# A residual's affine placed inside the FFN, and the rotary product issued one block later

## What is computed

```python
x = _layernorm(DEEPNORM_ALPHA * x + gt1 * y, ln1_g[i], ln1_b[i])
x = _layernorm(DEEPNORM_ALPHA * x
               + gt2 * _swiglu(x * (1.0 + sc2) + sh2, ffn_w_gate[i], ffn_w_up[i], ffn_w_down[i]),
               ln2_g[i], ln2_b[i])
# _layernorm(x, g, b) = (x - mean) * rsqrt(var + eps) * g + b
# in the attention: q and k of the latent tokens get  x * cos + x_rot * sin
```

## Time and profile before

| | us |
|---|---|
| median of 3 runs | 4185.95 (4185.85 to 4187.7) |
| span of the profiled execution | 4179.4 |
| PE busy | 3880.4 |
| DVE busy | 2160.6 |
| ACT busy | 1670.0 |
| GpSimd busy | 617.0 |

### The profile page before, as it was taken

One profiled execution on the slowest core, in us unless ns is written; L12 is line 12 of the kernel. 1 busy time (PEld: TensorE's weight loads), 2 busy tenths in 40 slices (PEclk: granted clock), 3 DMA queues, 4 the chain that ended last, 5 costly groups with the idle time before them and its releaser, 6 DMA issues.

```text
span 4179.4 us, 67654 instructions
## 1 busy us (share of the span) xinstructions
PE 3880.4 (93%) x28266; PEld 3183.4 (76%) x28266; DVE 2160.6 (52%) x3078; ACT 1670.0 (40%) x2711; POOL 617.0 (15%) x676
## 2 busy tenths in 40 slices
PE   6999999789999989987999899999999998899999
PEld 4877777668888867756788675778888877778887
DVE  3667754753222453377324654555665428655564
ACT  4445455422112341264223336544334435544333
POOL 0045555421000001003000000000210003000120
PEclk9999999888999999999999899999999999999999
DMA  5243454321211121103232320222223230312332
GB/s 162 79 144 125 157 163 153 108 88 61 71 61 61 58 81 61 41 1 112 84 98 91 66 81 11 83 91 72 97 95 108 81 111 4 133 62 82 101 101 81
DMA packets 235991, 367.67 MB, mean 88 GB/s; under 512 B 9811, under 2 KB 142630, under 8 KB 235302
## 3 DMA queue, kind: packets, MB, share of 16 engines
q1 hardware_dynamic: 217200, 300.49, 21.8%
q0 software_dynamic: 17936, 62.70, 4.9%
q10 hardware_dynamic: 550, 0.17, 0.0%
HBM read 344.36 MB, written 18.96 MB: 87 GB/s over the span
## 4 chain that ended last, share of the span: by engine, by line
PE 75%; DVE 15%; ACT 7%; issue 2%; DMA 1%; ACTq 0%; POOL 0%; DVEq 0%; SPq 0%; POOLq 0%
PE psum L259 21%; PE psum L261 20%; PE psum L260 20%; PE psum L256 12%; DVE arena L289 4%; ACT arena L389 3%; PE psum L265 2%; DVE arena L299 2%; DVE rw L289 2%; DVE rx L383 2%; DVE arena L303 1%; ACT rw L393 1%; DVE arena L295 1%; DVE arena L315 1%; ACT rx L393 1%
## 5 line engine op out<-in xcount | busy, mean ns | idle before, releaser
L259 PE MATMUL psum<-rx,rw 128*128 128x512 f32 (+2 forms) x2864 | 1057.8, 369 | 47.0 <-DVE rx L383 28.2
L260 PE MATMUL psum<-rx,rw 128*128 128x512 f32 (+2 forms) x2864 | 1030.5, 360 | 0.0
L261 PE MATMUL psum<-rx,rw 128*128 128x512 f32 (+2 forms) x2864 | 1028.6, 359 | 0.0
L289 DVE TENSOR_TENSOR rw<-arena,rw 128x2048 fp32r<-128x2048 f32 (+3 forms) x266 | 549.8, 2067 | 811.5 <-ACT rw L393 802.1
L256 PE MATMUL psum<-arena 32*32 32x32 f32 (+10 forms) x12982 | 762.8, 247 | 112.8 <-ACT arena L393 41.2
L256 PEld LDWEIGHTS psum<-arena 32*32 32x32 f32 (+5 forms) x12982 | 580.6, 133 | 256.1 <-issue 84.8
L393 ACT ACTIVATE rw<-arena 128x2048 fp32r<-128x2048 f32 (+3 forms) x266 | 453.6, 1705 | 753.4 <-PE psum L261 737.6
L259 PE MATMUL psum<-rw,rx 128*128 128x512 f32 (+1 forms) x1720 | 680.9, 396 | 31.1 <-DVE rx L383 13.8
L259 PEld LDWEIGHTS psum<-rx,rw 128*128 128x128 f32 (+1 forms) x2864 | 550.6, 192 | 181.8 <-DVE rx L383 40.6
L260 PE MATMUL psum<-rw,rx 128*128 128x512 f32 (+1 forms) x1720 | 672.5, 391 | 0.0
L261 PE MATMUL psum<-rw,rx 128*128 128x512 f32 (+1 forms) x1720 | 672.3, 391 | 0.0
(11 more groups left out here) (73 smaller groups left out, 2216.6 us busy)
## 6 DMA issues: line engine op xcount, KB each, us to landing
arena<-in_ffn_w_up SPq DMA_DIRECT2D x66, 1024.0 KB, 5.0
arena<-in_ada_w SPq DMA_DIRECT2D x48, 1024.0 KB, 6.6
arena<-in_ffn_w_down SPq DMA_DIRECT2D x40, 1024.0 KB, 4.9
arena<-in_ffn_w_gate SPq DMA_DIRECT2D x22, 1024.0 KB, 5.1
arena<-in_dn_w_in SPq DMA_DIRECT2D x16, 1024.0 KB, 6.0
arena<-in_xa_w_kv SPq DMA_DIRECT2D x16, 1024.0 KB, 5.0
arena<-in_hgrn_w_in SPq DMA_DIRECT2D x16, 1024.0 KB, 5.4
arena<-in_da_w_in SPq DMA_DIRECT2D x12, 1024.0 KB, 5.0
```

What stands on the lines that cost most here:

```text
L259: self.e.matmul(out, l[0], r[0], start=start, stop=False)
L260: self.e.matmul(out, l[0], r[1], start=False, stop=False)
L261: return self.e.matmul(out, l[1], r[0], start=False, stop=stop)
L289: return self.e.tensor_tensor(out, a, b, op)
```

## The change

`res1` and `res3` are unchanged in content, but GpSimd waits for `g0_GT 4` or `g1_GT 4` in front of them. `res2` is done a row (128 tokens) at a time in the attention's projection: behind cosine 6, 8, 10 and 12 GpSimd loads row t of `x_s`, multiplies and adds, and stores it back; the later reload brings the finished rows. The rotary product of block n is issued behind the first segment of block n+1, that of block 15 behind the first four-column step of the V projection. `have` becomes a function that gives the key.

```diff
-    v.wait_ge(*K.at(have, t))
+    v.wait_ge(*K.at(*have(t)))
+RES = DW + 3456
+def res_row(K, t):
+    return K.mem(RES + t % 2 * 1024, 1024)
+def pool_res_row(g, K, t):
+    gain, bias = pair_of(K, RES + 2048)
+    x = res_row(K, t)
+    if t == 0:
+        g.wait_ge(*K.at("m3_lo", 15))
+        pool_ln_rows(g, K, ("ln_rows", 2), RES + 2048, "ln2", 0)
+    if t >= 2:
+        g.wait_ge(*K.at("res_st", t - 2))
+    g.load(("res_ld", t), [(x, K.x_s[:, t * 1024:(t + 1) * 1024])], f"res_ld{t % 2}")
+    if t == 0:
+        g.wait_ge(*K.at("ln_rows", 2))
+    g.wait_ge(*K.at("res_ld", t))
+    g.tt(x, x, gain, MUL).then_inc(*g.sig())
+    g.tt(x, x, bias, ADD).then_inc(*g.sig(("res_x", t)))
+    g.wait_ge(*K.at("res_x", t))
+    g.load(("res_st", t), [(K.x_s[:, t * 1024:(t + 1) * 1024], x)], f"res_st{t % 2}")
+def pe_da_rot(p, K, n):
+    cosT, sinT, rot, raw, tmp = rope_mem(K, n)
+    p.wait_ge(*K.at("da_raw", n))
+    b = p.bank("da_rot", n)
+    p.mm(b[:, :], rot, raw).then_inc(*p.sig(("da_rot", n)))
+    p.close("da_rot", n)
@@ pe_da_proj
-            if s == 0:
-                cosT, sinT, rot, raw, tmp = rope_mem(K, n)
-                p.wait_ge(*K.at("da_raw", n))
-                b = p.bank("da_rot", n)
-                p.mm(b[:, :], rot, raw).then_inc(*p.sig(("da_rot", n)))
-                p.close("da_rot", n)
-    for j in range(2):
-        pe_proj_tok(p, K, ("da_v", j), da[:, 2048 + j * 512:2560 + j * 512], None, range(6))
+            if s == 0 and n:
+                pe_da_rot(p, K, n - 1)
+    pe_proj_tok(p, K, ("da_v", 0), da[:, 2048:2560], None, range(6), None,
+                lambda kh, t: pe_da_rot(p, K, 15) if (kh, t) == (0, 0) else None)
+    pe_proj_tok(p, K, ("da_v", 1), da[:, 2560:3072], None, range(6))
@@ pool_da_proj
+        if n == 15:
+            for t in (2, 3):
+                g.wait_ge(*K.at("res_st", t))
         g.tt((KT if wk else QT)[:, f, 0:512], raw, cosT, MUL).then_inc(*g.sig(("da_cos", n)))
+        if n in (6, 8, 10, 12):
+            pool_res_row(g, K, n // 2 - 3)
@@ dve_program: have="res1" / "res2" / "res3" become
+            have=lambda t: ("res1", t)    # down0
+            have=lambda t: ("res2",)      # da_out
+            have=lambda t: ("res3", t)    # down1
@@ pool_program
+    g.wait_ge(*K.at("g0_GT", 4))
     pool_affine(g, K, "res1", range(6), ("ln_rows", 1), CO + C_ONE, lambda t: ("m2_read", t // 4), K.X)
...
-    pool_ln_rows(g, K, ("ln_rows", 2), WK + 7168, "ln2", 0)
-    g.load(("x2",), [(da_rows(K), K.x_s.rearrange("p (t n) -> p t n", n=1024))])
-    pool_affine(g, K, "res2", range(4), ("ln_rows", 2), WK + 7168, lambda t: ("x2",),
-                da_rows(K))
+    g.load(("res2",), [(da_rows(K), K.x_s.rearrange("p (t n) -> p t n", n=1024))])
...
+    g.wait_ge(*K.at("g1_GT", 4))
     pool_affine(g, K, "res3", range(4), ("ln_rows", 3), WK + 18432, lambda t: ("m4_read", t // 2), K.X)
```

More of the change, by code:

```diff
@@ L4683, in dve_program @@
     dve_out(v, K, "down0", 22, 6, swiglu_out(K, 6), pair_of(K, CO + C_ONE), after=dve_ln_after(v, K, "ln2", t3),
-            have="res1")
+            have=lambda t: ("res1", t))
     yield "b0"
@@ L4693, in dve_program @@
     dve_ln_cols(v, K, "m4", 2, 1, 24, 32)
-    dve_out(v, K, "da_out", 8, 4, gate=pair_of(K, WK + 6144), after=dve_ln_after(v, K, "ln3", t4), have="res2",
+    dve_out(v, K, "da_out", 8, 4, gate=pair_of(K, WK + 6144), after=dve_ln_after(v, K, "ln3", t4), have=lambda t: ("res2",),
             begun=1, old=da_rows(K))
@@ L4701, in dve_program @@
     v.wait_ge(*K.at("gate_rows", 1, 1))
-    dve_out(v, K, "down1", 22, 4, out, pair_of(K, WK + 17408), after=dve_last_norm(v, K, WK + 20480), made=1, have="res3",
+    dve_out(v, K, "down1", 22, 4, out, pair_of(K, WK + 17408), after=dve_last_norm(v, K, WK + 20480), made=1, have=lambda t: ("res3", t),
             late=True)
```

## The result

The changed kernel takes **4127.34 us** (median of 4 runs, 4123.37 to 4134.16), the kernel before 4186.82 us beside it (4185.85 to 4188.02): ratio 0.9865, interval 0.9852 to 0.9878. The forecast was 4141 us with a range of 4134 to 4156.

What follows compares the result with a forecast made beforehand. TensorE, busy 93% of the span, bounds the kernel, so only its waits or low clock pay. Gains 14.7 + 11.2 + 3.6 + 15.6 = 45.1 us off 4179.4 give 4134.3, with 6.5 around the span 4141 us; range 4134 to 4156.

Steps and rivals of the forecast that it cites:

- part 4: Attention projection: issuing each rotary product a block later hides its ACT copy; gain 15.6 us, bounds 11 and 17.
- Part 1: Turn m2: moving res1 out frees DVE's splits from GpSimd's products; gain 9.0 + 5.7 = 14.7 us.
- part 2: Turn m4: moving res3 out shortens two halves on PE's path; gain 11.2 us.
- Part 3: Output projection: moving res2 out removes two PE waits; gain 3.6 us, bounds 2 to 5.
- (a): FFNs: moved res1 and res3 products delay weight splits by 4.9 us against 6.0 us of cover; cost 0.
- (b): Attention projection: res2's row 0 takes GpSimd 13 to 18 us against 22 us of room; hidden by 4 to 9.
- (c): Output projection start: x_s load and five broadcasts leave together, some 22 us sooner; cost 0, at worst a few us.
- (d): DVE's extra waits per tile name things long done; possible DMA starvation adds 2.3 to 4.6 us to row 0, hidden.
- Rival 1: FFNs: splits lose their cover as the block moves along with the products; 20 us come back, 4161 us; 8%.
- Rival 4: Attention projection: res2's row trips on GpSimd hold up PE, making the kernel slower, 4196 us; 6%.
- Rival 3: Turns m2 and m4: GpSimd goes early or isn't the cause of slowness; 26 us not gained, 4167 us; 4%.
- Rival 2: Attention projection: low clock in block 1 and DVE's queue cut the rotary gain to 5 us, 4152 us; 12%.

Runs made afterwards that it cites:

- e2: The changed kernel run again with no edit: 4128.28 us, ratio 0.9866 to the kernel before.
- e7: The changed kernel run a third time with no edit: 4133.92 us, ratio 0.9877 to the kernel before.
- e3: The kernel before with only the rotary product issued one block later, the three affines unmoved: 4160.45 us, ratio 0.9944.
- e4: The changed kernel with the rotary product put back behind its own segment, so only the affines are moved: 4155.36 us, ratio 0.9931.
- e8: The kernel before with only the two GpSimd waits in front of res1 and res3 added: 4156.48 us, ratio 0.9932.
- e9: The kernel before with each 128x1024 GpSimd affine product and sum issued as two of 128x512, nothing moved: 4159.86 us, ratio 0.9945.
- e5: The changed kernel with the second half of turn m3 put ahead of block 2's rope on DVE: 4123.25 us, ratio 0.9853.

## Why the prediction was wrong

Two steps failed, and together they don't account for all of the miss.

**The first: "with 6.5 4141 us".** I took the distance between the one profiled span (4179.4) and the median of three runs (4185.95) as time around the span. It is 1.8 us in every run whose span is on record. The other 4.7 us are the scatter between executions of one kernel. The 42 later runs of the kernel before have a median of 4182.7 and reach from 4175.8 to 4188.7. The profiled one, at about 4181.2 with 1.8 us around it, was a little quick, and the median of the three that I started from lay 3.3 us higher than that of the 42. With 1.8 the forecast would have been 4136, from the median of the 42 runs 4138. I gave the range no room for this, since three runs lay within 1.9 us.

**The second: the sum, 45.1, of which part 4 had 15.6.** The stages give 47.8 to 51.0 us, and part 4 gives 20.2. The term that failed is the eleven waits of blocks 5 to 15, put at 7.1 us, which gave 10.5.

Of the 13.7 us between 4141 and 4127.3, 3.3 are the high start and 2.7 to 5.9 the sum. The rest, some 5 to 8 us, no experiment assigns to a cause. That the first profile's span (4132.4) came within 2 us of the 4134.3 summed was luck: parts 1 and 4 gave 6.8 us more than forecast, and part 2, the untouched stages and the part before 901 us took all but 1.9 of them back.

**The sum, by its parts** (us, forecast, then traces):

| part | forecast | measured |
|---|---|---|
| 1, m2 first half | 9.0 | 9.1 |
| 1, m2 second half | 5.7 | 7.8 |
| 2, m4 | 11.2 | 9.9 to 10.9 |
| 3, output projection | 3.6 | 2.1 to 3.5 |
| 4, rotary | 15.6 | 20.0 to 20.2 |
| rest, untouched stages | 0 | −2.8 to +1.1 |
| sum | 45.1 | 47.8, 47.8, 51.0 |

- Part 1, first half: the model turn m3 was right to 0.1 us. Second half: mis-sized by 2.1 us. DVE's splits themselves gave the 5.4 us that I had read from the rows. I left out PE's matmuls behind them, which ran at the low clock after the waits. About the same work in before, then in the changed kernel:

```profile
975.00:980.00 5.00, 4.52 (x17) 3.94 (x18) 1.76 (x4) 2.21 (x5) 0.00 (x0) 0.50 0.77 208
980.00:985.00 5.00, 5.00 (x32) 5.00 (x32) 0.00 (x0) 1.50 (x2) 0.00 (x0) 0.71 0.00 0
...
961.00:966.00 5.00, 4.51 (x36) 4.13 (x35) 1.94 (x4) 2.35 (x5) 0.00 (x0) 1.00 0.00 0
966.00:971.00 5.00, 5.00 (x44) 5.00 (x44) 1.37 (x1) 2.30 (x2) 0.00 (x0) 1.00 0.00 0
```

  The granted clock is 0.50 and 0.71 in the first pair (0.50 is the lower level, 1.2 GHz) and 1.00 in the second. In two of three traces of the changed kernel 1.5 us of that were given back in front of the down projection: a wait of 5.4 us, which the change doesn't touch, was followed by a lower clock there (0.62 in 1310:1315 of e2, 0.88 in e7, which gave nothing back).
- Part 2: 9.9 to 10.9 us; the two halves came out up to 1.3 us smaller than 11.2, and why the traces differ by 1 us here is open.
- Part 3 went as worked out: the weight split takes 2.29 us again (1893.28 in the changed kernel), the evictions start with PE, both waits are gone; the 2.1 is e7, whose units before it were 1.6 us quicker than in the other two.
- Part 4: the failed term is "eleven waits of 0.65 to 0.69 us, 7.1 us"; it measured 10.5. Up to block 5 the working nearly holds: block 2 starts at 1525.42, where I had 1525.4 (counted from the start of the stage, which is 14.9 us earlier), and the wait in front of block 4, forecast at 3.1 us, is 3.3. But each of the eleven blocks became shorter by 0.96 us, not by 0.65 to 0.69. In the chain of before stand a copy and a product; in the chain of the changed kernel, a product:

```profile
1644.83 0.61 ACT arena L393
1645.48 1.12 PE psum L256 x2
...
1612.80 0.86 PE psum L256 x2
```

  The product costs 0.86 us on the chain when it follows the matmul before it without a stop, and 1.12 when it starts on a semaphore. A wait that goes takes the restart of the engine behind it along, 0.27 us for each block. That and the rounding down to 7.1 make 3.4 of the 4.6 us. About 1 us more came up to block 5, where product 3 was no longer waited for (10.5 us instead of 9.6), and 0.2 from block 15's product, 0.9 instead of 1.1.
- The costs at nothing: (a) hidden, as the FFN's window shows, with a blocked split of 4.53 us as in the earlier trace rows; (b) hidden (e3, e4), GpSimd away 10 to 14 us; (c) and (d) no new wait of PE in the output projection.
- Rivals 1 and 4 are excluded by e8 and e4. Rival 3 is excluded by e8, where the two waits alone give 26.9 us in m2 and m4, and by e9, where GpSimd's instructions alone are changed. Rival 2 had its mechanism right, the turn behind product 2, worth 5.1 us with e5; but my sum already had products 2 and 3 that far apart (11.4 us, measured 11.44). Block 1 did not run at the low clock (1516:1523 has a granted clock of 1.00).

**What stays open.** By stages the change is worth 47.8 to 51.0 us, by medians 49.5 to 59.5. The difference must lie in front of 901 us, where DVE, ScalarE and GpSimd have the same instructions in the same order in both kernels, or in executions that weren't profiled. Ten profiles of edited kernels stand at −5.9 to +4.5 us there, mean −1.7, the two of before at 0 and +1.0. That is too few against a spread of 10 us to say whether that part is really quicker or whether the first two sets of runs were lucky.

The best version is e5: moving the turn ahead on DVE costs one line and takes another 5 us by stages, twice 4123 us by median.

## What to carry to other kernels

An elementwise job on GpSimd beside a serial stage of DVE can cost every two-input instruction of DVE the length of one GpSimd instruction (up to 2.7 us instead of 0.69 here); put it beside a stage in which the matmuls have several microseconds of cover, or, where it can't move, cut its instructions shorter. When an instruction is held back to hide its wait, look at what stands behind its consumer on each other queue, as the turn did here. Before a gain of one per cent is forecast, measure how far two traces and ten runs of the unchanged kernel differ, and in which stage.

## What the runs showed that I had not expected

A wait costs more than its length: PE's 0.69 us for the copy were worth 0.96 us, since the rotary product behind it took 1.12 us instead of 0.86. Halving GpSimd's instructions alone, with the same elements at the same place, won 14.7 us by stages. And stages without any edit repeat to 0.1 us in some traces but jump by 1 to 3 us in others, with another granted clock behind the same wait or lull: 0.62 in one and 0.88 in another, 0.50 in one and 0.91 in another.
